# Router and token preparation inside the last out-projection, on tokens without their norm, in a two-layer encoder with experts

## What is computed

```python
def rms_norm(x, w):
    xf = x.astype(jnp.float32)
    y = xf * lax.rsqrt(jnp.mean(xf * xf, axis=-1, keepdims=True) + RMS_EPS)
    return (y * w.astype(jnp.float32)).astype(x.dtype)

    h = h + jnp.concatenate([y_dn, y_df, y_ml], axis=-1) @ w_out[l]
    u = rms_norm(h, ffn_norm_w[l])
    ...
    logits = (u @ router_w).astype(jnp.float32)
    top_vals, top_idx = lax.top_k(logits, TOP_K)
    gates = jax.nn.softmax(top_vals, axis=-1)
    for e in range(N_EXPERTS):
        out = out + combine[..., e:e + 1] * ((jax.nn.silu(u @ w_gate[e]) * (u @ w_up[e])) @ w_down[e])
    return h + out     # without the meta tokens
```

## Time and profile before

| | |
|---|---|
| median of 3 runs | 2046.8 us (2044.5 to 2047.6) |
| the profiled execution | 2047.8 us, span 2046.0 us |
| mean granted TensorE clock | 0.957 of full speed |
| busy share of the span: PE, DVE, ACT | 95%, 74%, 55% |
| DMA | 443.6 MB, mean 217 GB/s |
| last out-projection, first matmul to last | 972.6 to 1010.4 us |
| first matmul of the experts | 1041.0 us |

### The profile page before, as it was taken

One profiled execution on the slowest core, in us unless ns is written; L12 is line 12 of the kernel. 1 busy time (PEld: TensorE's weight loads), 2 busy tenths in 40 slices (PEclk: granted clock), 3 DMA queues, 4 the chain that ended last, 5 costly groups with the idle time before them and its releaser, 6 DMA issues.

```text
span 2046.0 us, 27032 instructions
## 1 busy us (share of the span) xinstructions
PE 1941.8 (95%) x10940; PEld 1654.7 (81%) x10940; DVE 1516.8 (74%) x1877; ACT 1122.4 (55%) x1236; POOL 73.9 (4%) x67
## 2 busy tenths in 40 slices
PE   7998989889999997988899999999999999999998
PEld 6986858789998985767878888888888888888886
DVE  7747585555546758675568888988889888898886
ACT  4542243343334543423367777777777777777775
POOL 1001111000000001112000000000000000000000
PEclk9995889899999996989899999999999999999999
DMA  9500000545536500001459999999999999999994
GB/s 304 155 26 1 1 1 1 190 143 172 167 122 181 160 27 0 1 1 62 170 218 363 351 351 351 357 348 359 350 351 353 348 362 344 359 351 366 365 354 184
DMA packets 139428, 443.61 MB, mean 217 GB/s; under 512 B 14369, under 2 KB 94289, under 8 KB 96161
## 3 DMA queue, kind: packets, MB, share of 16 engines
q1 hardware_dynamic: 138272, 437.87, 58.7%
q0 software_dynamic: 1024, 3.93, 0.5%
HBM read 439.61 MB, written 2.16 MB: 216 GB/s over the span
## 4 chain that ended last, share of the span: by engine, by line
PE 87%; DVE 9%; issue 1%; DMA 1%; ACT 1%; POOL 0%; DVEq 0%; POOLq 0%; ACTq 0%
PE ps L1781 22%; PE ps L1783 22%; PE ps L1782 22%; PE ps L2164 2%; PE ps L2149 2%; PE ps L2168 2%; PE ps L1794 2%; DVE cacc L1189 2%; DVE w_lo L1089 1%; PE ps L1943 1%; PE ps L2298 1%; PE ps L1990 1%; PE ps L2309 1%; PE ps L1806 1%; PE ps L2026 1%
## 5 line engine op out<-in xcount | busy, mean ns | idle before, releaser
L1146 DVE TENSOR_TENSOR m_lo<-raw,m_hi 128x2048 fp32r<-128x2048 f32 x336 | 768.4, 2290 | 144.9 <-ACT m_hi L777 144.9
L777 ACT ACTIVATE m_hi<-raw 128x2048 fp32r<-128x2048 f32 x336 | 644.2, 1918 | 274.6 <-PE ps L1783 274.6
L1781 PE MATMUL ps<-m_hi,xe_hi 128*128 128x512 f32 x896 | 358.5, 400 | 1.1 <-ACT xe_lo L1019 1.1
L1783 PE MATMUL ps<-m_lo,xe_hi 128*128 128x512 f32 x896 | 353.6, 395 | 0.0
L1782 PE MATMUL ps<-m_hi,xe_lo 128*128 128x512 f32 x896 | 353.6, 395 | 0.0
L1089 DVE TENSOR_TENSOR w_lo<-raw,w_hi 128x1024 fp32r<-128x1024 f32 (+1 forms) x164 | 183.4, 1155 | 124.4 <-ACT w_hi L742 124.3
L1781 PE MATMUL ps<-u_hi,w_hi 128*128 128x272 f32 x800 | 237.7, 297 | 14.7 <-DVE u_lo L1139 10.8
L1783 PE MATMUL ps<-u_lo,w_hi 128*128 128x272 f32 x800 | 233.7, 292 | 0.0
L1782 PE MATMUL ps<-u_hi,w_lo 128*128 128x272 f32 x800 | 232.5, 291 | 0.0
L742 ACT ACTIVATE w_hi<-raw 128x1024 fp32r<-128x1024 f32 (+1 forms) x164 | 159.6, 1002 | 124.7 <-PE ps L1783 124.7
L1783 PEld LDWEIGHTS ps<-m_lo,xe_hi 128*128 128x128 f32 x896 | 168.0, 187 | 41.1
(11 more groups left out here) (386 smaller groups left out, 2794.5 us busy)
## 6 DMA issues: line engine op xcount, KB each, us to landing
raw<-in_moe_units SPq DMA_DIRECT2D x336, 1024.0 KB, 4.9
raw<-in_w_in SPq DMA_DIRECT2D x30, 1024.0 KB, 5.5
raw<-in_w_out SPq DMA_DIRECT2D x16, 768.0 KB, 5.3
raw<-in_ffn_w_gate SPq DMA_DIRECT2D x11, 1024.0 KB, 5.1
raw<-in_ffn_w_up SPq DMA_DIRECT2D x11, 1024.0 KB, 5.2
raw<-in_ffn_w_down SPq DMA_DIRECT2D x8, 896.0 KB, 5.0
raw<-in_ffn_w_down SPq DMA_DIRECT2D x4, 1024.0 KB, 5.2
w_uq<-in_mla_w_uq SPq DMA_DIRECT2D x2, 768.0 KB, 4.3
```

The lines of the kernel that those rows point to most:

```text
L777: nc.scalar.activation(m_hi[k % RING][:, :], raw[:, slot, :], ACT.Copy).then_inc(m_hi_ready, 1)
L1146: V.tensor_tensor(m_lo[k % RING][:, :], raw[:, mslot(k), :], m_hi[k % RING][:, :].bitcast(F32), ALU.subtract).then_inc(m_lo_ready, 1)
L1781: mm(o, w[0], x[0], start=first, stop=False)
L1783: return mm(o, w[0], x[1], start=False, stop=last)
```

## The change

Nothing of the expert weights' handling changes. The tokens are no longer normed before the router and the gather. DVE weighs each quarter of `h` by the norm's weight alone (`weigh`, gives `hw`), behind each group's addition. PE does the router matmuls, the transposes of `hw` and those of `h` for a quarter in `tokens(k)`: `tokens(0)` behind the second group, `tokens(1)` behind the third, `tokens(2)` and `tokens(3)` behind the fourth. ACT makes `x_hi`, `acc` and the sums of squares of a token (`token_sq`, a square with an accumulated sum, now with the token on the partition) in `token_parts(k)`; DVE makes `x_lo` in `token_low(k)`. The sums, the root and the weighing of before fall away in this layer. `lo(0)` moves ahead of the last addition, `lo(1)` to `lo(3)` behind the selection; `hi(1)` and `hi(2)` behind the token work.

The choice of experts works on logits without the norm. The reciprocal root (`token_r`) is made during the first gathers; it scales the difference of the two logits ahead of the gate exponential, and matmuls with `sel` (`slot_r`) bring it to the slots, where `silu` takes it as its scale and `hidden` as a factor. The two high copies of the first gathers stay on ACT, the two low ones go to DVE. The count for `crowd`, the gate exponential, the load of the silu table and `router_gates` move behind the first gathers, beside the first units. `first_max` has one step less (a second constant row `iota16`), the position one less, since the constant row counts from 1.

```diff
+            def token_parts(k):
+
+                S = fr_act
+                cs = slice(2 * P * k, 2 * P * k + 2 * P)
+                two = lambda b: ps[:, b, :].rearrange("p (t n) -> p t n", t=2)
+                fr_pe.wait(act, 0, "x", k)
+                S.mark(nc.scalar.activation(x_hi[:, :, cs], two(TURNED[0]), ACT.Copy), "x", k)
+                fr_pe.wait(act, 0, "h", k)
+                S.mark(nc.scalar.activation(acc[:, :, cs], two(TURNED[1]), ACT.Copy), "h", k)
+                if k:
+                    S.wait(act, 0, "sq", k - 1)
+                for t in range(2):
+                    i = nc.scalar.activation(eg[:, 2 * P * t:2 * P * t + 2 * P], two(TURNED[1])[:, t, :], ACT.Square, accum_out=token_sq[:, t, k:k + 1])
+                S.mark(i, "sq", k)
...
+                out_last = [groups[g][1][-1] for g in plan[l]["out"]]
+                if l == DEPTH - 1:
+                    hi_upto(out_last[2])
+                    fr_act.begin(0)
+                    token_parts(0)
+                    hi_upto(out_last[3])
+                    token_parts(1)
+                    hi(0)
+                    token_parts(2)
+                    token_parts(3)
+                    hi(1)
+                    hi(2)
+                    continue
...
                 act.wait_ge(eh_ready, pas * (LAST + 1) + n)
-                nc.scalar.activation(eg[:, :], ps[:, 0, :], ACT.Silu).then_inc(silu_done, 1)
+                e, c = divmod(n, CHUNKS)
+                if c == 0 and e == 0:
+                    act.wait_ge(slot_r_ready, pas + 1)
+                elif c == 0 and e % 2 == 0:
+                    act.wait_ge(gslot_ready, pas * PAIRS + e // 2 + 1)
+                nc.scalar.activation(eg[:, :], ps[:, 0, :], ACT.Silu, scale=slot_rows[:, e // 2 % 2, 2 + e % 2:3 + e % 2]
+                                     ).then_inc(silu_done, 1)
...
+                first_xe_high(pas, 0)
+                if pas == 0:
+                    S = fr_act
+                    fr_dve.wait(act, 0, "norms")
+                    nc.scalar.activation(token_r[:, :], token_r[:, :], ACT.Ln, bias=cols[:, 60:61], scale=1.0 / D).then_inc(log_taken, 1)
+                    act.wait_ge(log_taken, stat[0] + 1)
+                    S.mark(nc.scalar.activation(token_r[:, :], token_r[:, :], ACT.Exp, scale=-0.5), "rstd")
+                first_xe_high(pas, 1)
+                if pas == 0:
+                    fr_dve.wait(act, 0, "top")
+                    S.mark(nc.scalar.activation(rcol[:, 4:6], rcol[:, 4:6], ACT.Exp), "gate_exp")
+                    nc.scalar.preload_act_table_set("silu_and_others")
...
+                def weigh(k):
+
+                    for kt in (2 * k, 2 * k + 1):
+                        i = V.tensor_scalar(hw[:, kt, :], h[:, kt, cso], p_(C_FFN + kt), None, ALU.mult)
+                    fr_dve.mark(i, "hw", k)
+
+                def token_low(k):
+
+                    fr_act.wait(dve, 0, "x", k)
+                    cols_k = slice(2 * P * k, 2 * P * k + 2 * P)
+                    fr_dve.mark(V.tensor_tensor(x_lo[:, :, cols_k], ps[:, TURNED[0], :].rearrange("p (t n) -> p t n", t=2),
+                                                x_hi[:, :, cols_k].bitcast(F32), ALU.subtract), "x", k)
...
+                if l == DEPTH - 1:
+                    fr_dve.begin(0)
+                    fr_dve.mark(V.tensor_scalar(rl[:, 9, :, :], bc(iota[:, 0:NEXP], 1, 2), -16.0, None, ALU.add), "iota")
                 for k, g in enumerate(plan[l]["out"]):
                     lo_upto(min(groups[g][1][-1] + 1, groups[plan[l]["out"][-1]][1][-1]))
+                    if l == DEPTH - 1 and k == 3:
+                        lo(0)
                     add_to_h(g, k)
+                    if l == DEPTH - 1:
+                        weigh(k)
+                        if k:
+                            token_low(k - 1)
...
+            token_low(3)
             fr_pe.wait(dve, 0, "rank")
-            link(V.tensor_tensor(incl, ps[:, 0, 0:16].rearrange("p (t e) -> p t e", t=2), msk, ALU.mult))
-            for p_i in range(2):
-                V.tensor_scalar(posp[:, p_i, :, :], incl, -1.0 - P * p_i, None, ALU.add)
-            S.mark(V.tensor_copy(gates[:, :, :], comb), "slots")
...
-                V.tensor_tensor(eh[:, :], eg[:, :], ps[:, 1, :], ALU.mult).then_inc(eh_ready, 1)
+                e = n // CHUNKS
+                V.scalar_tensor_tensor(eh[:, :], ps[:, 1, :], slot_rows[:, e // 2 % 2, 2 + e % 2:3 + e % 2], eg[:, :],
+                                       ALU.mult, ALU.mult).then_inc(eh_ready, 1)
...
                 select(pas, 0)
+                if pas:
+                    lo(MOE_UNITS)
+                lo(pas * MOE_UNITS + 1)
+                first_xe_low(pas, 0)
+                first_xe_low(pas, 1)
+                if pas == 0:
+                    router_norms()
+                lo(pas * MOE_UNITS + 2)
+                if pas == 0:
+                    router_margin()
+                first_slot_r(pas)
+                lo(pas * MOE_UNITS + 3)
+                if pas == 0:
+                    router_gates()
...
+            def tokens(k):
+
+                fr_dve.wait(pe, 0, "hw", k)
+                if k == 3:
+                    logits(k)
+                if k:
+                    fr_dve.wait(pe, 0, "x", k - 1)
+                turned_tokens(k, "x", TURNED[0])
+                if k:
+                    fr_act.wait(pe, 0, "sq", k - 1)
+                turned_tokens(k, "h", TURNED[1])
+                if k < 3:
+                    logits(k)
+
+            for k, g in enumerate(plan[DEPTH - 1]["out"]):
+                stream(g, (y_hi, y_lo), slice(META, T))
+                if k == 1:
+                    pe.wait_ge(log_taken, stat[0])
+                    pe.wait_ge(router_in, 16)
+                if k:
+                    tokens(k - 1)
+            tokens(3)
             fr_dve.wait(pe, 0, "mask")
             msk = rl[:, 6, :, :]
             mm(ps[:, 0, 0:8], mat(M_TRI), msk[:, 0], start=True, stop=True)
             mm(ps[:, 0, 8:16], mat(M_TRI), msk[:, 1], start=True, stop=False)
-            mm(ps[:, 0, 8:16], ones, msk[:, 0], start=False, stop=True)
-            mm(ps[:, 0, 16:24], ones, msk[:, 0], start=True, stop=False)
-            S.mark(mm(ps[:, 0, 16:24], ones, msk[:, 1], start=False, stop=True), "rank")
-            pe.wait_ge(crowd_ready, 1)
-            fr_act.wait(pe, 0, "h", 3)
+            S.mark(mm(ps[:, 0, 8:16], ones, msk[:, 0], start=False, stop=True), "rank")
...
+                if p:
+                    i = slot_r(2)
                 i.then_inc(sel_turned, 1)
+
+            def slot_r(c0):
+                for x in range(2):
+                    for t in range(2):
+                        i = mm(ps[:, GATHER[0], c0 + x:c0 + x + 1], sel[:, t, P * x:P * x + P].bitcast(F32),
+                               token_r[:, t:t + 1], start=(t == 0), stop=(t == 1))
+                return i
...
+                for i, step in enumerate((0, 2, 1, 3)):
+                    if i == 3:
+                        pe.wait_ge(xe_ready, pas * XE + 1)
+                    gather(pas, 0, step, (FIRST_GATHERS[i], FIRST_GATHERS[i] + 1))
                 for n in range(LAST + 1):
                     e, c = divmod(n, CHUNKS)
                     k0 = pas * MOE_UNITS + chunk_units(n)
                     x = tuple(v[e // 2 % 2][:, :, P * (e % 2):P * (e % 2) + P] for v in (xe_hi, xe_lo))
-                    if e % 2 == 0 and c == 0:
-                        pe.wait_ge(xe_ready, 4 * (pas * PAIRS + e // 2 + 1))
+                    if n == 0:
+                        pe.wait_ge(xe_low_ready, 2 * pas + 1)
+                    elif e % 2 == 0 and c == 0:
+                        pe.wait_ge(xe_ready, pas * XE + 2 + 4 * (e // 2))
                     if n or pas:
                         pe.wait_ge(silu_done, pas * (LAST + 1) + n)
-                    wide(k0, x, 0)
+                    wide(k0, 0, x, 0)
+                    if n == 0:
+                        if pas == 0:
+                            fr_act.wait(pe, 0, "rstd")
+                        slot_r(0).then_inc(slot_r_turned, 1)
+                        if pas == 0:
+                            fr_act.wait(pe, 0, "sq", 3)
+                            mm(ps[:, TURNED[1], 0:NEXP], ones, msk[:, 0], start=True, stop=False)
+                            S.mark(mm(ps[:, TURNED[1], 0:NEXP], ones, msk[:, 1], start=False, stop=True), "crowd")
+                        pe.wait_ge(xe_ready, pas * XE + 2)
+                        pe.wait_ge(xe_low_ready, 2 * pas + 2)
+                    wide(k0 + 1, 1, x, 0)
```

More of the change, by code:

```diff
@@ L2314, in turn_sel @@
                 pe.wait_ge(sel_ready, pas * PAIRS + p + 1)
+                if pas == 0 and p == 0:
+                    fr_dve.wait(pe, 0, "slots")
+                    pe.wait_ge(crowd_ready, 1)
+                if p == 0:
+                    pe.wait_ge(slot_r_ready, pas + 1)
                 for x in range(2):
```

199 lines of the change are left out of this document (99 added, 100 removed).

## The result

| | before | after |
|---|---|---|
| median, in one comparison | 2047.7 us (6 runs) | 2033.2 us (6 runs, 2032.2 to 2038.5) |
| ratio | | 0.9928, 95% interval 0.9912 to 0.9943 |
| the profiled execution | 2047.8 us, span 2046.0 | 2035.4 us, span 2033.6 |
| mean granted TensorE clock | 0.957 | 0.966 |
| busy share: PE, DVE, ACT | 95%, 74%, 55% | 95%, 75%, 55% |

The change is faster. In this comparison it saved 14.7 us (0.9928 of 2046.8 is 2032.1) where 9.5 were forecast, and 2032.1 lies just outside the range of 2033 to 2043. Two later comparisons gave 0.9958 and 0.9945.

The account below looks back on a forecast made before the run. PE bounds the experts' stage, so an earlier first expert matmul shortens the end: 15.1 us earlier, less 1.3, 0.8, 1.0 and 2.5, gives 9.5; 2047.8 - 9.5 = 2038.3 profiled, 2037.4 median. Range for 8 in 10: 2033 to 2043.

Parts of the forecast that it names:

- (1): First chunk of the experts: PE also does `slot_r` (0.82 us) and the crowd count (0.44), a loss of 1.3 us.
- (2): First chunk: weight splits now lie beside the first units, `lo(3)` ends at 23.6, so PE waits 0.8 us.
- (3): First chunk: `hidden(0)` queues on DVE behind `router_gates` and `lo(4)`; PE waits 1.8 us against 0.84, 1.0 lost.
- (4): Later expert pairs: three `turn_sel` each have 8 more narrow instructions on PE, 2.5 us lost.
- (5): All 56 chunks: per-row factor in `silu` and `hidden`, at most 0.1 us each, off the path, nothing lost.
- moment 0: The moment at which the last out-projection matmul is issued, 1010.36 us before the change; forecast to move 2.3 us later.
- rival (a): Half clock falls in the first expert units or lasts longer: 2039 to 2043, chance 0.12; no fall: gathers 1.7 us shorter.
- (b): Rival: token work woven into the out-projection holds it up, 1 to 2 us at three boundaries: 2040 to 2043, chance 0.08.
- (c): Rival: first chunk worse than forecast, a new wait for m_lo, PE waits 2 us longer: 2039.5, chance 0.09.
- (d): Rival: slot factor in `silu` and `hidden` gets onto PE's path, 0.3 us per chunk: 2054, slower than before, chance 0.03.
- (e): Rival: waits push all four `tokens` behind the last out-projection matmul, 3.5 us more there, 2.2 less ahead: 2039 to 2041, chance 0.03.
- better than 2034.5: Case: clock up in the gathers and the first chunk's two waits gone, 1.7 + 1.8 us; chance 0.05.

Follow-up runs that it names:

- the filled kernel: Changed kernel plus constant matmuls into an unused bank ahead of PE's waits for the mask (5) and the selection (3): ratio 0.9937, stretch 2.5 us less than after.
- the second set of constant matmuls: Kernel before plus constant matmuls in PE's waits for the token norm (13), first x_lo (4) and selection matrix (6): ratio 0.9995, stretch 1.8 us less.
- the first set: Kernel before plus constant matmuls in PE's waits for the token norm (13) and the selection matrix (8): ratio 1.0015, stretch 3.5 us more.

## Why the prediction was right and wrong

**What failed: the step from the sum to the number.** It is the paragraph on the number, and the range behind it. It took the one profiled execution less 9.5 us, which is the median of three runs less 9.5, and built the lower end of the range, 2033, from mechanisms of the changed code alone. It had no term for the code ahead of the change, whose length differs by 4 us between executions of one kernel (959.3 to 963.3 at the last `o_dn` of the changed one), nor for medians over few runs; the 4.1 us that it says can be told apart went into the chances of faster and slower, not into the range. The 14.7 us measured first are 10.5 of the change and about 4 of that spread; over the 23 runs of the three comparisons the ratio 0.9947 gives 2036.0, 1.4 us from the 2037.4 forecast. That the sum came so near is in part luck: it had too much in the out-projection and in the two waits (0.45, 0.6 and 0.8 us) and too little in the gathers, the chain ahead of them and the later `slot_r` (0.55, 0.1 and 0.2), and the errors partly cancel. A range for a total must hold the spread of the unchanged part, even where the edit is priced to 1 us.

The terms of the sum, by their numbers in the forecast:

| term | forecast | measured | |
|---|---|---|---|
| out-projection longer | 2.3 | 1.85 | a `tokens(k)` is 1.68, not 1.75; the rest of the difference has no row |
| last out-projection matmul to mask | 5.5 | 5.4 | |
| to the selection | 7.5 | 7.75 | |
| the gathers | 5.5 | 6.05 | mis-sized |
| to the first expert matmul | 13.2 | 13.86 | from the gathers |
| (1) `slot_r` and the count | 1.3 | 1.3 | |
| (2) wait for `lo(3)` | 0.8 | about 0.2 | mis-sized |
| (3) wait for `eh`, more than before | 1.0 | 0.2 | mis-sized |
| (4) three later `slot_r` | 2.5 | 2.7 | |
| (5) the factors | 0 | 0 | |
| sum | 9.5 | 10.5 | |

The chain behind moment 0 was right to 0.3 us up to the first gather (7.8 against 7.7 us). The gathers were taken from the nearest row, with a stretch of half clock inside. PE's pauses ahead of them were as forecast (1.8 and 1.2 us with 1.1 us of narrow work between, for 1.8 and 1.4), but the half clock lay on more of the gathers than in that row. Before, then after:

```profile
1034.33:1039.86 5.53, 5.53 (x32) 5.33 (x32) 0.00 (x0) 2.95 (x3) 0.00 (x0) 0.69 0.01 3
```

```profile
1018.18:1024.24 6.06, 6.05 (x33) 6.06 (x33) 3.38 (x2) 1.89 (x2) 0.00 (x0) 0.60 0.45 164
```

The gain would be 2.2 us more at full clock, as the filled kernel shows, close to the 1.7 that rival (a) gave for it.

The waits of the first chunk were priced too high, though the chains on ACT and DVE ran to time. The gate exponential was forecast for 18.0 behind moment 0 and started at 17.9 (1028.31), `lo(3)` for 21.2 and started at 21.4 (1031.77). But PE, late by the gathers, was through with units 0 to 2 at 23.6 instead of 22.9, just as `lo(3)` ended. For `eh` the forecast had PE ready at 26.5 and `hidden(0)` done at 28.2, which is a wait of 1.7 and not the 1.8 that it goes on with; it was 26.8 and 27.8. DVE was 0.4 us earlier because `router_gates` and the crowd count took 1.24 us and not 1.65: not every step of theirs costs 0.206. So the gathers' loss and the smaller waits are partly one thing: a delay ahead of a chain that runs on two other engines is paid once. The first chunk as a whole is 1.7 us longer than before (14.40 for 12.72), where items 1 to 3 had 3.1.

None of the rivals came about. (a): the clock fell ahead of the gathers, as the sum had it, and stayed out of the expert units (1.00 from 1024 on), so that only 0.55 us more were lost; its price for three units at half clock, 2 x 2.8, should have been 3 x 2.8 by its own row. (b): PE has no wait inside the out-projection behind its first. (c): PE waited less in the first chunk than the sum had. (d): `hidden` and `silu` cost PE nothing. (e) was tried: with the weave undone the stretch is 0.7 us longer (about 1.2 with equal gathers), where the forecast gave it 1.6 to 3.6. The first comparison's 2032.1 would fit the case of better than 2034.5, but for another reason: the clock was not up, and of the 1.8 us that it gave for the two waits of the first chunk 1.4 came.

## What to carry to other kernels

Here a chain between two streams of matmuls was shortened by taking steps off it, the norm and what the selection doesn't need, far more than by weaving its work into the stream ahead: a quarter cost PE 1.7 us woven and 2.1 to 2.3 in a block, and the weave was worth about 1 us of 10.5. Before buying clock or speed on one engine, look at what the next engine in the chain is doing: three quarters of what the router gained on PE were lost to weight splits already queued on DVE. And a gain of 10 us in 2 ms needs the stage's own stretch from several traces, because the total of few runs was off by 4 us here from code that nobody touched.

## What the hardware showed that was not expected

A square with an accumulated sum on ACT is a square (0.39 us for 256 columns) and a separate instruction of 0.21 us; a quarter's token work is 1.8 us. With constant matmuls in the waits ahead of the gathers the granted clock stayed at 1.00 (1.1 us instead of 2.1 for eight gather matmuls), but where the clock was at 0.50 they took 0.84 us each instead of 0.44 and overran. And the clock fell while PE was busy by the profile's count. Windows of the kernel before with the second set of constant matmuls:

```profile
1020.00:1023.00 3.00, 3.00 (x26) 3.00 (x26) 3.00 (x3) 0.00 (x0) 0.00 (x0) 0.87 0.53 161
1023.00:1026.00 3.00, 3.00 (x17) 3.00 (x17) 2.76 (x9) 1.43 (x3) 0.00 (x0) 0.56 1.02 391
```

PE was busy for all of both windows and was granted 0.87 and then 0.56. A mean of 0.87 over 3 us is 0.8 us at half clock, so the fall lies near 1022.2, while the router's 32 instructions of 8 columns ran (1019.11 to 1023); during the constant matmuls of 256 columns ahead of them it had been granted 1.00. The kernel with the first set shows the same: busy for all of its window of 1020 to 1023, granted 0.73 in it, so the fall lies near 1021.4, and its router matmuls ran from 1018.2 to 1022.2. Whether the narrow matmuls are the cause was not tried.
